# Applying a norm weight after the gather instead of before it, in the expert stage of a hybrid-MoE block followed by two SWA/GLA layers

## What is computed

```python
e_prob = jax.nn.softmax(e_logits, axis=-1)
top_p, top_i = lax.top_k(e_prob, TOP_K_EXPERTS)
top_w = g_gate[:, None] * top_p / jnp.sum(top_p, axis=-1, keepdims=True)
...
for e in range(N_EXPERTS):
    hid = jax.nn.silu(t @ w_gate[e]) * (t @ w_up[e])
    out = out + combine[:, e:e + 1] * (hid @ w_down[e]).astype(F32)
```

## Time and profile before

| | |
|---|---|
| median of three runs | 2520.03 us (2517.58 to 2520.05) |
| the profiled execution | 2520.5 us, its span 2518.6 us |
| PE busy | 2313.8 us, 92% |
| DVE, ACT, POOL busy | 1485.1, 1156.6, 424.3 us |
| mean granted PE clock | 0.959 |

### The profile page before, as it was taken

How to read it: one execution, slowest core, us unless ns; L and a number is a source line. 1 busy time by engine, 2 the same in 40 slices (tenths; PEclk the granted TensorE clock), 3 DMA queues, 4 the chain that set the end, 5 groups by cost and what they waited for, 6 DMA issues and landing times.

```text
span 2518.6 us, 29086 instructions
## 1 busy us (share of the span) xinstructions
PE 2313.8 (92%) x9901; PEld 1650.1 (66%) x9901; DVE 1485.1 (59%) x1501; ACT 1156.6 (46%) x1174; POOL 424.3 (17%) x151
## 2 busy tenths in 40 slices
PE   6899995999999999989987889999899978889997
PEld 4344544566566565558877766788688777667886
DVE  6966337888888888855545434455455464424554
ACT  4122414666666766643324546433343244464332
POOL 2640000000000000010005456300100053555000
PEclk8899997999999999999988999999999998999999
DMA  5234252999999999945543243555355432434652
GB/s 211 67 117 131 87 178 103 354 368 366 363 363 360 369 361 360 383 156 182 183 133 102 88 132 132 168 184 183 118 196 187 136 126 74 134 117 142 201 184 91
DMA packets 166450, 496.80 MB, mean 197 GB/s; under 512 B 10272, under 2 KB 21792, under 8 KB 136400
## 3 DMA queue, kind: packets, MB, share of 16 engines
q1 hardware_dynamic: 164528, 491.70, 55.2%
q10 hardware_dynamic: 1616, 3.24, 0.4%
q0 software_dynamic: 208, 0.59, 0.1%
HBM read 494.45 MB, written 1.05 MB: 197 GB/s over the span
## 4 chain that ended last, share of the span: by engine, by line
PE 66%; issue 14%; DVE 10%; POOL 6%; ACT 3%; DVEq 0%; DMA 0%; ACTq 0%; POOLq 0%
PE ps L967 11%; PE ps L968 11%; PE ps L969 11%; PE ps L1347 9%; PE ps L1018 6%; POOL w_lo L3041 6%; PE ps L1328 5%; PE ps L1332 5%; PE ps L1038 1%; PE ps L1316 1%; PE ps L1109 1%; PE ps L1385 1%; DVE W_r L2704 1%; ACT w_hi L1790 1%; PE ps L1364 1%
## 5 line engine op out<-in xcount | busy, mean ns | idle before, releaser
L3041 POOL TENSOR_TENSOR w_lo<-raw,w_hi 128x2048 fp32r<-128x2048 f32 x72 | 335.1, 4672 | 1599.8 <-ACT w_hi L1592 1404.5
L1592 ACT ACTIVATE w_hi<-raw 128x2048 fp32r<-128x2048 f32 (+1 forms) x204 | 378.9, 1865 | 459.2 <-PE ps L969 414.2
L967 PE MATMUL ps<-w_hi,a_hi 128*128 128x512 f32 (+1 forms) x1216 | 476.4, 392 | 54.7 <-POOL w_lo L3041 29.9
L968 PE MATMUL ps<-w_lo,a_hi 128*128 128x512 f32 (+1 forms) x1216 | 466.9, 384 | 0.0
L969 PE MATMUL ps<-w_hi,a_lo 128*128 128x512 f32 (+1 forms) x1216 | 465.3, 383 | 0.0
L2065 DVE TENSOR_TENSOR w_lo<-raw,w_hi 128x2048 fp32r<-128x2048 f32 (+1 forms) x132 | 293.1, 2227 | 264.4 <-ACT w_hi L1592 257.2
L967 PEld LDWEIGHTS ps<-w_hi,a_hi 128*128 128x128 f32 x1216 | 236.1, 194 | 105.9 <-POOL w_lo L3041 32.6
L969 PEld LDWEIGHTS ps<-w_hi,a_lo 128*128 128x128 f32 x1216 | 235.3, 194 | 44.4
L968 PEld LDWEIGHTS ps<-w_lo,a_hi 128*128 128x128 f32 x1216 | 236.2, 194 | 40.8
L1328 PE MATMUL ps<-w_hi,W_r 128*128 128x512 f32 x468 | 190.8, 408 | 5.4 <-DVE w_lo L2704 4.7
L967 PE MATMUL ps<-w_hi,y_hi 128*128 128x512 f32 x384 | 156.8, 408 | 18.4 <-DVEq L2530 18.4
(11 more groups left out here) (404 smaller groups left out, 3747.6 us busy)
## 6 DMA issues: line engine op xcount, KB each, us to landing
raw<-in_w_in SPq DMA_DIRECT2D x56, 1024.0 KB, 5.1
raw<-in_ffn_w_gate SPq DMA_DIRECT2D x44, 1024.0 KB, 5.1
raw<-in_ffn_w_up SPq DMA_DIRECT2D x44, 1024.0 KB, 5.1
raw<-in_ffn_w_down SPq DMA_DIRECT2D x40, 1024.0 KB, 5.0
raw<-in_w_up SPq DMA_DIRECT2D x30, 1024.0 KB, 7.9
raw<-in_w_gate SPq DMA_DIRECT2D x30, 1024.0 KB, 7.1
lo_f<-in_w_up SPq DMA_DIRECT2D x30, 1024.0 KB, 8.1
lo_f<-in_w_down SPq DMA_DIRECT2D x29, 1024.0 KB, 7.6
```

The source lines that it names most:

```text
L967: pe.matmul(dst, a_h, b_h, start=first, stop=False, **kw)
L968: pe.matmul(dst, a_h, b_l, start=False, stop=False, **kw)
L1592: act.activation(E.view(w_hi, name), E.view(raw, name), ACT.Copy).then_inc(hi_split, 1)
L3041: pool.tensor_tensor(E.view(w_lo, name), E.view(raw, name), E.view(w_hi, name).bitcast(F32), ALU.subtract)\
```

## The change

It leaves the norm weight out of the token rows. The rows that are gathered are now `x` times the inverse root alone; PE gathers the high and the low part into the same 256 columns of a bank, and on the way out the value is multiplied by the weight, which is then one number for each partition (`gain_f`, loaded by eight DMAs of 128 single numbers each, issued by ACT). ACT writes the rounded product, and DVE afterwards the rest; DVE's instruction frees the bank. The row-shaped weight and `xn` are gone. `h_rows` is written in the order of the blocks, so that its writes have a step of 256 elements (1 KB) while `x_sb` is read straight on. ACT rounds the weights of the first gate and up tiles ahead of the norm, and POOL makes their low parts (four more instructions of 128x2048 on POOL, four fewer on DVE). The first gate product stands ahead of `slot_weights` on PE, and `spots` stands behind the gather's copies on DVE.

```diff
+                        at = slice(kb % 4 * SEQ + kb // 4 * P, kb % 4 * SEQ + kb // 4 * P + P)
+                        m = pe.matmul(dst[:, 0:SEQ], h_rows[half][:, t, at], pick[:, t, :], start=half == 0 and t == 0,
+                                      stop=half == 1 and t == 1, skip_group_check=True)
...
+                for a in range(4):
+                    for h in range(2):
+                        act.dma_start(gain_f[32 * a:32 * a + 32, 4 * h:4 * h + 4], gain_src[a][:, h]).then_inc(gain_loaded, 16)
...
-            act.wait_ge(done["residual"], nth("residual", ("wo", 1, 1)))
-            stats("f", x_sb, junk_f)
+            for name in FIRST_TILES[0:2]:
+                for half in range(2):
+                    expert_rounded(name, half)
             for t in range(2):
-                act.wait_ge(done["normed"], nth("normed", t))
-                act.activation(h_rows[0][:, t], xn[:, t], ACT.Copy).then_inc(done["row_hi"], 1)
+                act.wait_ge(done["residual"], nth("residual", ("wo", 1, t)))
+                act.activation(junk_f, x_sb[:, t, :], ACT.Square, accum_out=st_ss[:, t:t + 1]).then_inc(scalar_step, 1)
+                act.wait_ge(scalar_step, step.next())
+            inverse_root("f", st_ss, r_of["f"], D)
+            for t in range(2):
+                act.activation(by_block(h_rows[0][:, t]), in_order(x_sb[:, t]), ACT.Copy, scale=r_of["f"][:, t:t + 1])\
+                    .then_inc(done["row_hi"], 1)
                 act.wait_ge(done["row_hi"], nth("row_hi", t))
...
-            def gathered_copy(name, kb, group):
+            def gathered_hi(name, event, kb, group):
                 act.wait_ge(bank_filled[bank_of[name]], fills(name))
+                act.activation(packed_rows[group][:, kb, :, 0:SLOTS], psum(name)[:, 0:SEQ].rearrange("p (q s) -> p q s", s=SLOTS),
+                               ACT.Copy, scale=gain_f[:, kb:kb + 1]).then_inc(done["gathered_hi"], 1)
+                act.wait_ge(done["gathered_hi"], nth("gathered_hi", event))
...
                 for t in range(2):
                     dve.wait_ge(done["row_hi"], nth("row_hi", t))
-                    tt(h_rows[1][:, t], xn[:, t], h_rows[0][:, t].bitcast(F32), ALU.subtract).then_inc(done["row_lo"], 1)
+                    stt(out=by_block(h_rows[1][:, t]), in0=in_order(x_sb[:, t]), scalar=r_of["f"][:, t:t + 1],
+                        in1=by_block(h_rows[0][:, t]).bitcast(F32), op0=ALU.mult, op1=ALU.subtract).then_inc(done["row_lo"], 1)
                     dve.wait_ge(done["row_lo"], nth("row_lo", t))
-                dve.memset(hid_e[SLOTS:P], 0.0).then_inc(vector_step, 1)
...
             def gathered(name, event, kb, group):
-                evacuate(name, packed_rows[group][:, kb].rearrange("p q (h s) -> p h q s", h=2),
-                         psum(name).rearrange("p (h q s) -> p h q s", h=2, q=GROUP_TILES))
+                dve.wait_ge(done["gathered_hi"], nth("gathered_hi", event))
+                rows = packed_rows[group][:, kb]
+                stt(out=rows[:, :, SLOTS:P], in0=psum(name)[:, 0:SEQ].rearrange("p (q s) -> p q s", s=SLOTS),
+                    scalar=gain_f[:, kb:kb + 1], in1=rows[:, :, 0:SLOTS].bitcast(F32), op0=ALU.mult, op1=ALU.subtract)\
+                    .then_inc(bank_freed[bank_of[name]], 1)
+                dve.wait_ge(bank_freed[bank_of[name]], fills(name))
                 dve.sem_inc(done["gathered"], 1)
...
+            for name in FIRST_TILES[0:2]:
+                for half in range(2):
+                    u = (name, half)
+                    pool.wait_ge(expert_hi, E.split_number(u) + 1)
+                    pool.tensor_tensor(E.expert_raw(u)[1], E.expert_raw(u)[0], E.expert_hi(u).bitcast(F32), ALU.subtract)\
+                        .then_inc(expert_lo, 1)
             pool.wait_ge(done["residual"], nth("residual", ("wo", 1, 1)))
```

More of the change, by code:

```diff
@@ L62 @@
            "relued maxed exped probs probs_turned branch gates residual route_in route silu hidden "
-           "hidden_turned masks places spots tables normed row_hi row_lo picked gathered gathered_act lower summed gated "
+           "hidden_turned masks places spots tables row_hi row_lo picked gathered gathered_hi lower summed gated "
            "expert_hidden expert_turned spread out_hi out_split scattered gate_ln decay decay_exp decayed gk_turned masked state columns").split()
@@ L345, in plan @@
         fill(("G", "first", 0, kb), kb % 4)
-    mark("gathered", *(("first", 0, kb) for kb in range(0, KB, 2)))
-    mark("gathered_act", *(("first", 0, kb) for kb in range(1, KB, 2)))
+    for signal in ("gathered_hi", "gathered"):
+        mark(signal, *(("first", 0, kb) for kb in range(KB)))
     expert_unit(("g", "first")); expert_unit(("u", "first")); expert_unit(("g", "second"))
@@ L1415, in experts @@
                     gather(("G", "first", 0, kb), kb)
+                pe.wait_ge(done["gathered"], nth("gathered", ("first", 0, KB - 1)))
+                expert_rows(("g", "first"), 0, 0)
                 pe.wait_ge(done["spots"], nth("spots", 0))
@@ L1769, in _ @@
             act.dma_start(iota, A["head_rows"][0:SEQ].partition_broadcast(P)).then_inc(tables_loaded, 16)
+            at_gain = P + 2 * KB
+            gain_src = A["packed"][:, at_gain:at_gain + KB].rearrange("(b k) (h a) -> a b h k", k=4, a=4)
+            with nc.allow_non_contiguous_dma(reason="the gain in the order of the expert rows"):
+                for a in range(4):
+                    for h in range(2):
+                        act.dma_start(gain_f[32 * a:32 * a + 32, 4 * h:4 * h + 4], gain_src[a][:, h]).then_inc(gain_loaded, 16)
             for hh in range(2):
@@ L2488, in _ @@
                     dve.sem_inc(done["gained"], 1)
[L2490 to L2510 removed]
+            dve.memset(hid_e[SLOTS:P], 0.0).then_inc(vector_step, 1)
+            dve.wait_ge(vector_step, step.next())
             def hidden(k, dst, gate_, w, weight):
@@ L2793, in experts @@
                 expert_lower(("g", "second"), 1)
+                for kb in range(2):
+                    gathered(("G", "first", 1, kb), ("first", 1, kb), kb, 1)
                 regs["moe"] = 0
```

82 lines of the change are left out of this document (23 added, 59 removed).

## The result

The changed kernel takes 2535.99 us (median of 6 runs, 2533.54 to 2537.82) where the kernel before takes 2519.90 (6 runs beside them, 2516.97 to 2520.77): a ratio of 1.0064, 95% interval 1.0053 to 1.0074. It is 16 us slower, where 6 us faster was forecast, and it lies outside the range.

The account below looks back on a forecast made before the run. PE was taken to bound the loop and DVE's program the passage into it. The terms -1.4 + 1.3 - 7.4 - 3.1 + 4.4 gave -6.2 against 2520.5 us: 2514.3, range 2511.5 to 2517.

Parts of the forecast that it names:

- A: Router start ahead of the loop: DVE loses copies and normed rows, PE's product may run at half clock; -1.4 us.
- B: Low rows up to `places`: writes with a 1 KB step make DVE's instructions longer, 2.2 us each; +1.3 us.
- C: Gather's start to first gate product: 14.3 us shrinks to 6.85, with POOL's low parts done in time; -7.4 us.
- D: First gate product to the loop's first up product: PE stays at full clock, 23.8 us becomes 20.7; -3.1 us.
- E: Expert loop: two added DVE instructions a period lengthen PE's eight waits for `picked`; +4.4 us with the first periods' delay.
- VectorE becomes the bound: Rival, expert loop: added DVE instructions of 1.2 us each would pace all 32 periods; 2526 us, chance 0.05.
- The early part gives nothing: Rival, passage: half clock through the router product and low rows at 5.5 us; -2.6 us, 2518, chance 0.27.
- POOL late: Rival, ahead of the loop: POOL's four low parts run past 372 us or hold DVE; 2518 us, chance 0.03.
- steps are free: Rival: low rows at 2.5 us, router product at full clock, little lost at `picked`; -12.6 us, 2508, chance 0.17.
- F: Loads: eight ACT issues of single numbers fall into ACT's idle time, SP's loads move with PE's releases; nothing.

Follow-up runs that it names:

- a body of 268: Changed kernel with leaner signals and one-hot rows made earlier (252 instructions in VectorE's loop), plus 16 long-passed waits there; 2516.54 us.
- the 252-instruction kernel: Changed kernel with leaner signals on VectorE in the loop and one-hot rows made ahead of the last low-weight step; 2499.44 us.
- the two kernels whose loops pay nothing: Kernel before and changed kernel, each with leaner VectorE signals and one-hot rows made earlier; 2511.43 and 2499.44 us.

## Why the prediction was wrong

**A, router start, -1.4.** The mechanism was the one named: PE, without `gain_row`, stands for 2.29 us and the product of 36 columns runs at 0.50. It takes 6.25 us, not twice 3.76, as its first part was at the full clock. The routing's first reduction comes at 382.60 against 383.46 in the trace of before: -0.9.

**B, low rows, +1.3.** 1.98 us each for 2.2: +0.8 up to `places`. A and B together: 392.74 against 392.77, 0.0 where -0.1 was forecast. The step of 1 KB costs what the normed rows' 16 bytes cost, a little less.

**C, -7.4.** 398.80 to 405.83 is 7.03 us, against 14.28: -7.25. POOL's four parts ended at 365.2, each 4.50 long.

**D, -3.1.** The loop's first up product came at 428.70, not at 426.5: 22.9 us from the gate product instead of 20.7, -1.0. Up to the last half of the second gate product the steps are the forecast ones (8.3 and 8.1 us for 8.0 and 8.2). The last piece is the miss: 6.4 us where 4.5 stood for it. It ran at 0.50 from its start at 422.26 to past 427. I had let PE stay at the full clock because it would be idle for under 2 us; its idle times were 1.84 us, behind which the clock stayed full, and 1.88, behind which it fell at 417.8, before the wait of 2.01 began.

**The passage's sum:** -8.2 at the first up product for -10.6, both misses being clock.

**E, in the loop, +4.4: the step that failed.** It measured +26.6: 15.4 at `picked` and 11.1 at the branches back. Its price of an instruction was right: 0.484 us, as the nearest row had it. So was where it would be felt: at `picked`, where PE's waits grew by 6.3 us in sum, for 4.0, inside the ends of 1.6 and 7.4 (by its own terms the upper end is 8 x 0.85 + 0.4 = 7.2). Two things stood on no line of it.

The first: a wait was priced at its own length. Six of the eight passed from 1 us to 1.8 to 2.0 and the clock behind them fell, so that the 6.3 us of wait cost 15.4. The order of two steps removes it all (2535.99 to 2522.68, with the stops growing meanwhile).

The second, which no rival had: 41 more instructions in the body. DVE's work in it was counted, and its code was not. Two stops a trip of 3 to 4 us each, three times, cost PE 11.1 us here and 22 to 25 where nothing else held it. It is shown from both sides: put into the kernel before as empty waits, the 41 instructions bring the two stops and cost 14.5 us in all; taken out of the changed kernel at the same work, the length gives back the branches' 19.1 us (22.1 with the early order); and 16 empty waits bring the stops back. The Trainium skill, "Runtime: NRT & Kernel Launch", section "Instruction fetch mechanics", says that a taken branch whose target is not in the engine's window has to fetch it before it goes on; the packets at each branch agree. It gives that window as two blocks, 512 instructions in all; here a body of 268 was too long and one of 261 was not, and the measurement decides.

The rival **VectorE becomes the bound** had the sign by chance: 2526, from every period growing. Periods without `picked` or a branch kept 17.0 us, and the 252-instruction kernel has PE at 100.00 us of 100 with all gathered steps in. **The early part gives nothing** was nearest in the passage (half clock at the router). **POOL late** didn't happen, nor did **steps are free**. F was nothing, as forecast.

Between the two kernels whose loops pay nothing, the change is worth 9.5 us up to the loop's first transposes, where the forecast had 10.6 up to the first up product.

## What to carry to other kernels

Count a loop body's instructions on each engine as well as its microseconds: waits, signals and register steps are instructions too, and a body that grew past its limit shows in three places at once: "issue" at the first instruction behind the branch, packets on the instruction queue in steady state, and the first period of a trip longer (in one run the second too). A signal that only repeats a freed bank can be dropped to pay for an instruction that does work. A wait on PE near 1 us isn't worth its length alone: before adding to what is ahead of it, move the step that it waits for, as here, where one step of 4 instructions placed ahead of one of 2.3 us gave 9 us to the old kernel and 13 to the new.

## What the runs showed of the hardware that was not expected

- A body of 261 instructions on VectorE ran through its branches with no instruction packet at all; with 268 to 302 the engine stood 6.5 to 8.0 us behind each, in two stops. What sets the number, and whether another engine has the same, was not tried. ACT's body has 233 to 245 instructions in these runs, below the number; PE's shows 512 matmuls, 512 weight loads and some 110 others and has no such stop.
- The granted clock isn't decided by the last wait's length alone. In the changed kernel it stayed full behind PE's waits of 1.49 us at 480.84, 1.84 at 405.83, 2.47 at 722.54 and 2.13 at 868.91, and fell to half behind those of 1.77 at 550.75, 1.88 at 417.10, 2.29 at 375.93 and 2.75 at 577.00. What PE did before each differs, and these runs don't part the two.
- Waits on a long passed value aren't free on VectorE: five instructions of two such waits each in a period moved `picked` by about 0.5 us, some 0.1 us for each instruction.
